# Hybrid GLA + sliding-window layer: the product of queries and states per head on 64 rows, instead of block-diagonal pairs

## The reference, cut to what matters

```
q_in  = q * exp(b)                  k_in = k * exp(-b)
inter = q_in @ S                    # (tokens x 64) @ (64 x 128), per head: the product that is changed
A     = (q_in @ k_in.T) * causal    # per head
intra = A @ v                       # (tokens x tokens) @ (tokens x 128), per head
o     = inter + intra
S     = exp(b_end) * S + k_out.T @ v
o_gla = rmsnorm(o) * silu(gate)
```

## Time and profile before

| what | value |
|---|---|
| median of 3 runs | 1670.41 us (1670.38 to 1670.56) |
| profiled execution, its own time | 1671.04 us |
| its span, first to last instruction | 1669.0 us |
| TensorE (PE) busy | 1589.3 us, 95% of the span |
| weight loads (PEld) busy | 931.4 us, 56% |
| VectorE (DVE) busy | 1012.7 us, 61% |
| ScalarE (ACT) busy | 661.6 us, 40% |
| GpSimd (POOL) busy | 425.1 us, 25% |
| mean granted TensorE clock | 0.976 of 2.4 GHz |

### The profile page before, as it was taken

The page is one execution under the profiler, slowest core; times in us unless marked ns, Lnnn a source line. Parts: engine busy times, 40 slices in busy tenths (PEclk is TensorE's granted clock), DMA queues, the critical chain, the costliest instruction groups (busy, mean ns, idle before and its releaser), DMA issues.

```text
span 1669.0 us, 30516 instructions
## 1 busy us (share of the span) xinstructions
PE 1589.3 (95%) x12071; PEld 931.4 (56%) x12071; DVE 1012.7 (61%) x1711; ACT 661.6 (40%) x1983; POOL 425.1 (25%) x439
## 2 busy tenths in 40 slices
PE   8277899999999999999999999999999999999995
PEld 3135455565656655655566666565556666655553
DVE  1257655666666666566666666665667666665555
ACT  0254344344434444434443444444344334444432
POOL 0111222222232233222323223222222232332221
PEclk9679899999999999999999999999999999999998
DMA  8944322222222222212222222122212222221312
GB/s 272 297 121 96 102 59 57 44 64 62 69 69 69 64 68 57 63 45 61 58 69 69 69 69 63 57 69 48 53 57 69 69 69 69 63 67 53 86 24 68
DMA packets 233894, 127.77 MB, mean 77 GB/s; under 512 B 181853, under 2 KB 221286, under 8 KB 233862
## 3 DMA queue, kind: packets, MB, share of 16 engines
q1 hardware_dynamic: 224422, 124.16, 27.6%
q10 hardware_dynamic: 9440, 3.17, 0.9%
HBM read 49.23 MB, written 17.59 MB: 40 GB/s over the span
## 4 chain that ended last, share of the span: by engine, by line
PE 89%; DVE 3%; issue 2%; DMA 1%; ACT 1%; POOL 0%; ACTq 0%; SPq 0%; POOLq 0%
PE bank L455 55%; PE pairP L455 21%; PE pairQ L634 2%; PE bank L548 2%; PE bank L544 2%; PE bank L568 1%; PE pairQ L555 1%; PE pairQ L603 1%; DMA hT<-h_tok 1%; PE bank L579 1%; PE bank L596 1%; PE bank L646 1%; PE pairQ L607 0%; PE bank L642 0%; DVE etmp L1143 0%
## 5 line engine op out<-in xcount | busy, mean ns | idle before, releaser
L455 PE MATMUL bank<-w_hi,hT 128*128 128x512 f16 (+1 forms) x2640 | 751.2, 361 | 32.1 <-DMA hT<-h_tok 31.4
L455 PE MATMUL bank<-w_lo,hT 128*128 128x512 f16 (+1 forms) x1320 | 475.7, 360 | 0.0
L455 PEld LDWEIGHTS bank<-w_hi,hT 128*128 128x128 f16 x2640 | 258.9, 98 | 291.9 <-DMA hT<-h_tok 31.7
L455 PE MATMUL pairP<-wo_hi,late 128*128 128x512 f16 x1056 | 322.3, 382 | 10.6 <-issue 6.4
L455 PE MATMUL pairP<-wo_lo,late 128*128 128x512 f16 x528 | 201.6, 382 | 0.0
L455 PEld LDWEIGHTS bank<-w_lo,hT 128*128 128x128 f16 x1320 | 129.7, 98 | 114.3 <-issue 1.9
L455 PE MATMUL bank<-hT,w_hi 128*128 128x128 f16 x2112 | 183.4, 221 | 3.2 <-DVE w_lo L919 3.2
L455 PE MATMUL bank<-hT,w_lo 128*128 128x128 f16 x1056 | 181.0, 221 | 0.0
L455 PEld LDWEIGHTS pairP<-wo_hi,late 128*128 128x128 f16 x1056 | 104.0, 98 | 134.0 <-issue 10.2
L1182 POOL TENSOR_TENSOR xs<-xs,shift_row 128x1024 f32<-128x1024 f32 x33 | 79.6, 2411 | 351.0 <-DVE xs L937 351.0
L455 PEld LDWEIGHTS bank<-hT,w_hi 128*128 128x128 f16 x2112 | 162.7, 99 | 5.4 <-issue 3.3
(11 more groups left out here) (210 smaller groups left out, 2236.6 us busy)
## 6 DMA issues: line engine op xcount, KB each, us to landing
x_res<-x_in SPq DMA_DIRECT2D x33, 512.0 KB, 3.5
x_in<-in_x_prompt SPq DMA_DIRECT2D x32, 512.0 KB, 3.2
out<-stage SPq DMA_DIRECT2D x32, 512.0 KB, 2.6
w_hi<-in_w_ada SPq DMA_DIRECT2D x5, 1024.0 KB, 9.2
w_lo<-in_w_ada SPq DMA_DIRECT2D x5, 1024.0 KB, 13.0
wo_lo<-in_w_in SPq DMA_DIRECT2D x5, 1024.0 KB, 11.8
wo_hi<-in_w_in SPq DMA_DIRECT2D x3, 1024.0 KB, 11.1
stage<-in_w_ada SPq DMA_DIRECT2D x2, 1024.0 KB, 11.4
```

Of the source, the lines that this page charges most:

```text
L455: last = pe.matmul(out, a(c, i), b(c, j), start=(c == 0 and n == 0), stop=(c == KC - 1 and n == 2))
```

## The change

The block-diagonal product is split by head. Each head's product takes its own 64 rows of `q_int` and of `S` and 128 moving columns. The heads with q = 0 go to the first 256 columns of bank7, the heads with q = 1 to the first 256 columns of pairQ, which is another bank. The readers on ScalarE and VectorE follow. Since pairQ holds the scores, the wait for `p_exp` moves ahead of the o group. The zero quarters of `S` are no longer read by TensorE; they stay where they are.

```diff
+        o_ps = [bank7[:, 0:2 * DV].rearrange("p (b v) -> p b v", b=2), pairQ[:, 0:2 * DV].rearrange("p (b v) -> p b v", b=2)]
...
                     pe.wait_ge(sem["v_ev"], t)
+                    pe.wait_ge(sem["p_exp"], t)
                     if not c.second:
                         pe.wait_ge(sem["s_upd"], t - 1)
                     st = S_s if c.after else S
                     for b in range(2):
-                        pe.matmul(bank7[:, 2 * b * DV:2 * (b + 1) * DV], q_int[:, b, :], st[:, b, :, :],
-                                  start=True, stop=False)
+                        for q in range(2):
+                            r = slice(DK * q, DK * (q + 1))
+                            pe.matmul(o_ps[q][:, b, :], q_int[r, b, :], st[r, b, q, :], start=True, stop=False)
                         for q in range(2):
                             o = slice((2 * b + q) * DV, (2 * b + q + 1) * DV)
-                            last = pe.matmul(bank7[:, o], aT[:, b, q, :], v_tok[:, o], start=False, stop=(q == 1))
+                            last = pe.matmul(o_ps[q][:, b, :], aT[:, b, q, :], v_tok[:, o], start=False, stop=True)
                     last.then_inc(sem["o_mm"], 1)
 
                     n = DEC_SEQ if c.after else P
-                    pe.wait_ge(sem["p_exp"], t)
...
-                        last = act.activation(junk[:, hd * DV:(hd + 1) * DV], bank7[:, hd * DV:(hd + 1) * DV], ACT.Square,
+                        last = act.activation(junk[:, hd * DV:(hd + 1) * DV], o_ps[hd % 2][:, hd // 2, :], ACT.Square,
...
-                        last = dve.scalar_tensor_tensor(gates[:, o], bank7[:, o], o_r[:, hd:hd + 1], gates[:, o],
+                        last = dve.scalar_tensor_tensor(gates[:, o], o_ps[hd % 2][:, hd // 2, :], o_r[:, hd:hd + 1], gates[:, o],
```

## The result

The changed kernel takes 1682.95 us (median of 4 runs, 1682.43 to 1683.28), the kernel before 1670.49 us in the same job (4 runs): a ratio of 1.0074, 95% interval 1.0056 to 1.0091. It is slower by 12.5 us; the forecast was 1682.5 us. The profiled execution took 1683.15 us.

The account below looks back on a forecast made before the run. TensorE's stream was taken to bound the kernel. Per b, shape changes 0.19 plus loads 0.22 minus overlap 0.215 us gave +0.195; over 31 steps +12.1 us on the median 1670.41, so 1682.5 us, range 1675 to 1690.

Parts of the forecast that it names:

- What bounds it: Steps 2 to 32: TensorE's order alone sets the end; what its stream gains or loses arrives whole in the time.
- Overlap of the heads: Split product in the o group: the two heads run fully side by side, saving 0.215 us for each b.
- Price of a change of shape: Between 128-row and 64-row matmuls: 0.095 us each way, two changes or 0.19 us for each b.
- First load behind a change: At the first head's product and the first L548 behind it: exposed f32 weight load, 0.11 us each, 0.22 per b.
- Sum: O group: 0.19 + 0.22 - 0.215 = +0.195 us for one b, +0.39 us for one step.
- Which steps pay: Steps 1 and 33 are covered by other waits; steps 2 to 32 pay whole, 31 x 0.39 = +12.1 us.
- The wait moved, and the readers: Wait for `p_exp` ahead of the o group, and ScalarE and VectorE reading from two banks: both taken to cost nothing.

Follow-up runs that it names:

- the run with 128 rows and two banks: Changed kernel, but each head's product takes all 128 rows of queries and state again; two banks, moved wait and readers stay: 1672.02 us, 1.0011 of before.

## Why the prediction was right, point by point

*What bounds it.* Right: the stream of TensorE set the end before and after, and between 200 and 1600 us the changed kernel has no wait of a matmul, and none of a weight load on another engine. The 1.6 us of the earlier trace rows are gone too.

*Overlap of the heads.* Right: 0.01 us between the starts, and 0.217 us per block when it is taken away (0.215 forecast).

*Price of a change of shape.* Right: 0.09 us in and out. The Trainium skill, page "TensorEngine Tiling (Array Packing)", "Key Properties", speaks of a drain at each change of mode, not at each change of tile; the runs agree (0.01 us between heads, 0.09 us at each change) and add that it is paid for each change, not for each product.

*First load behind a change.* Right in kind and nearly in size: 0.10 and 0.11 us, against 0.11 taken from a load after idle.

*Sum.* 0.195 us per block was forecast. The o group grew by 0.37 us (0.185 per block) and the period by 0.357: over 31 steps 11.1 us, not 12.1. The forecast was 1 us above, for two reasons. The prices came out a little lower than taken (31 x 0.02 = 0.6 us). And the prediction left the six waits of the earlier trace rows as they were, but they went. Of before:

```profile
483.53 0.43 PE bank L544 x2
529.77 0.43 PE bank L544 x2
535.78 0.10 PEld L455 LDWEIGHTS bank<-w_hi,hT 128*128 128x128 f16 x1 [0.27 <-DVE gates L1006]
576.08 0.43 PE bank L544 x2
```

A step of before takes 46.24 us, and the six in which the load of that projection waits take 46.31; all 30 periods of the changed kernel are 46.61. So each step grew by the 0.37 us of its o group, and 6 x 0.07 = 0.4 us came back in all. Why the waits went was not tried.

*Which steps pay.* Step 1: its later waits are still there, 4.37 and 6.06 us against 4.11 and 6.36.

```profile
167.95 1.03 PE L605 MATMUL pairQ<-ident,etmp 128*128 128x128 f16 x8 [4.37 <-DVE junk L1042]
...
175.47 0.59 PE L456 MATMUL pairP<-wo_hi,late 128*128 128x512 f16 x1 [6.06 <-issue]
```

Step 33, timeline, against the earlier trace rows: `o_r` is over at 1651.16 us and VectorE comes to L1008 at 1653.69, so 2.5 us of cover are left of 2.7.

```profile
1650.96 0.20 ACT L676 ACTIVATE o_r<-o_ln 128x4 f32<-128x4 f32 x1
1653.69 0.34 DVE L1008 SCALAR_TENSOR_TENSOR gates<-bank,o_r,gates 128x128 f32<-128x128 f32 x1
```

*The wait moved, and the readers.* Right: the run with 128 rows and two banks holds both and costs 0.5 us in the steps.

*What fitted by luck.* The two profiled spans differ by 12.1 us, the 31 steps by 11.1. The missing 1 us is at the very end (the start of step 2 moved by only 0.18 us): the last output projection, 48 matmuls, took 11.95 us in the profile before and 13.14 in this one:

```profile
1659.67 13.14 PE pairP L456 x48
```

By stretches of 4 us (us, busy us of the engines, granted clock, DMA share, GB/s), both kernels ran its first part at half clock, 1.2 GHz, the changed one for longer. The first two lines are of before, whose projection starts at 1648.75 us:

```profile
1648.00:1652.00 4.00, 3.25 (x9) 1.22 (x10) 0.00 (x0) 0.00 (x0) 0.00 (x0) 0.54 0.02 3
1652.00:1656.00 4.00, 4.00 (x21) 1.77 (x19) 0.00 (x0) 0.00 (x0) 0.00 (x0) 1.00 0.00 0
...
1660.00:1664.00 4.00, 4.00 (x11) 1.43 (x10) 0.00 (x0) 0.00 (x0) 0.00 (x0) 0.50 0.02 4
1664.00:1668.00 4.00, 4.00 (x18) 1.71 (x17) 0.00 (x0) 0.00 (x0) 0.00 (x0) 0.88 0.00 0
```

Ahead of it TensorE had been waiting in both, busy for 1.8 us of the 8 us from 1652 to 1660 in the changed kernel and for 1.5 us of the 8 us from 1640 to 1648 before. The same projection took 13.31 us in the profile of the run with 128 rows and two banks, whose steps cost nearly as much as before, and 13.04, 12.12, 13.48 and 12.17 us in the other four. So it doesn't go with the added work.

The time ahead of step 2 moves too: in that run the state update product of step 2 starts at 205.88 us, 2.0 us earlier than before (207.85). So the parts outside steps 2 to 32 differ by 1 to 2 us from profile to profile. The steps explain 11.1 of the 12.5 us between the medians, and 0.5 of the 2 us of that run. The rest may come from these parts; the timed executions have no such rows, so that stays open. That the median comes within 0.5 us of the forecast, though the steps brought 1 us less, is luck.

## What to carry to other kernels

A product on half of the array wins its overlap only against two changes of shape and the first load behind each: at 2.4 GHz here 0.09 us and, for 128 f32 columns, 0.10 us, so two heads of two 128-column f32 passes (0.217 us won) lose when they stand alone among 128-row matmuls. Collect the products of one shape and put them next to matmuls that leave the full shape anyway, as the state update product did: the same matmuls then went from 1.0074 to 0.9967 of before. And price such an edit from the starts in the timeline around any matmul on a part of the array that the kernel already has.

## What the runs showed of the hardware that was not expected

No row of the kernel before could tell two things. Going from row halves to column halves or from quarters to column halves costs as much as coming from the full array (0.59 us for the state update product in all three cases). And four parts of the array at work at once stream 128 f32 columns at the pace of one (0.22 us for eight matmuls).
